# The attention layer's input product in 24 steps of seven products, W_v split beside the weight fusion, and one q, k, v tile loaded ahead

## What is computed

```
h = x @ w_in                       # 1024 x 3088: q 512, k 512, v 1024, g 1024, lr 16
gk = log_sigmoid(lr @ w_gk + b_gk) / 16          # per head, summed along each chunk
qe = q * exp(cumsum(gk)) ; ke = k * exp(-cumsum(gk)) ; kd = k * exp(last - cumsum(gk))
o = tril(qe @ ke.T) @ v + qe @ state             # state from chunk to chunk
y0 = (rmsnorm(o) * norm_w * silu(g)) @ w_out     # then a layer norm of ALPHA * x + y0
layer 1: h = x @ w_in ; causal means of u over 2, 4, 8, 16 rows ; @ w_grp ; * silu(z) ; @ w_out
```

## Time and profile before

| | us |
|---|---|
| median of three runs | 2005.64 |
| the profiled execution | 2001.48 |
| its span | 1999.6 |
| `prepare` to its last matmul | 132.3 |
| v in `project` | 132.3 to 313.0 |
| gate columns | 313.0 to 329.6 |
| four heads | 329.6 to 690.7 |
| start of `attend_and_norm`, to its first output product | 690.7 to 724.2 |
| last stage, its first matmul of a step | 1041.5 |

### The profile page before, as it was taken

How to read it: one execution, slowest core, us unless ns; L and a number is a source line. 1 busy time by engine, 2 the same in 40 slices (tenths; PEclk the granted TensorE clock), 3 DMA queues, 4 the chain that set the end, 5 groups by cost and what they waited for, 6 DMA issues and landing times.

```text
span 1999.6 us, 24456 instructions
## 1 busy us (share of the span) xinstructions
PE 1914.5 (96%) x8974; PEld 1588.5 (79%) x8974; DVE 1161.7 (58%) x1539; ACT 701.3 (35%) x1065; POOL 431.5 (22%) x268
## 2 busy tenths in 40 slices
PE   8999999999999989999949999999999999999997
PEld 7778887888888778888738888887888886787786
DVE  4330102332415277787675688868678657546998
ACT  4441213131313243343354444344434335224331
POOL 0005200000000000000043666423334343322430
PEclk9999999999999999999979999999999999999999
DMA  8766530334233464455322444333322225647342
GB/s 254 221 202 239 178 103 17 108 87 118 79 101 87 159 242 164 172 187 170 136 96 74 153 141 152 135 104 137 129 88 73 94 74 193 249 170 272 129 177 95
DMA packets 229912, 287.74 MB, mean 144 GB/s; under 512 B 17216, under 2 KB 170176, under 8 KB 227904
## 3 DMA queue, kind: packets, MB, share of 16 engines
q1 hardware_dynamic: 225216, 278.20, 42.0%
q10 hardware_dynamic: 4608, 8.39, 1.1%
HBM read 186.93 MB, written 99.61 MB: 143 GB/s over the span
## 4 chain that ended last, share of the span: by engine, by line
PE 41%; DVE 4%; issue 4%; ACT 1%; POOL 0%; DVEq 0%; POOLq 0%; ACTq 0%
PE banks L165 13%; PE banks L166 13%; PE banks L167 13%; DVE m_w_lo L1922 1%; DVE m_x_lo L1936 1%; ACT m_x_hi L1728 0%; DVE m_x_lo L1914 0%; PE banks L1621 0%; PE banks L1668 0%; DVE m_stats L2025 0%; DVE m_x_lo L1896 0%; DVE m_res L2019 0%; DVE m_res L2035 0%; POOL m_s L1859 0%; DVE m_win_b L1968 0%
## 5 line engine op out<-in xcount | busy, mean ns | idle before, releaser
L165 PE MATMUL banks<-m_x_hi,m_w_hi 128*128 128x512 f32 x1320 | 517.6, 392 | 9.4 <-DVE m_res L2019 3.5
L166 PE MATMUL banks<-m_x_lo,m_w_hi 128*128 128x512 f32 x1320 | 515.3, 390 | 0.0
L167 PE MATMUL banks<-m_x_hi,m_w_lo 128*128 128x512 f32 x1320 | 515.0, 390 | 0.0
L165 PEld LDWEIGHTS banks<-m_x_hi,m_w_hi 128*128 128x128 f32 x1320 | 248.7, 188 | 63.7 <-DVE m_w_lo L1922 10.0
L166 PEld LDWEIGHTS banks<-m_x_lo,m_w_hi 128*128 128x128 f32 x1320 | 248.8, 188 | 52.0 <-issue 0.7
L167 PEld LDWEIGHTS banks<-m_x_hi,m_w_lo 128*128 128x128 f32 x1320 | 248.7, 188 | 52.0
L1854 POOL TENSOR_TENSOR m_s<-pair_raw 128x512 f32<-128x512 f32 x24 | 47.3, 1969 | 891.6 <-POOLq L947 757.5
L165 PE MATMUL banks<-x_hi,h_w_hi 128*128 128x512 f32 x512 | 199.9, 390 | 0.8 <-DVE h_g_out L833 0.8
L166 PE MATMUL banks<-x_lo,h_w_hi 128*128 128x512 f32 x512 | 199.3, 389 | 0.0
L167 PE MATMUL banks<-x_hi,h_w_lo 128*128 128x512 f32 x512 | 199.3, 389 | 0.0
L1716 ACT ACTIVATE m_w_hi<-m_s 128x512 fp32r<-128x512 f32 x184 | 115.5, 629 | 202.7 <-PE banks L167 179.2
(11 more groups left out here) (220 smaller groups left out, 3117.7 us busy)
## 6 DMA issues: line engine op xcount, KB each, us to landing
p_in<-in_pool_w_in SPq DMA_DIRECT2D x32, 256.0 KB, 4.9
p_rows<-in_x SPq DMA_DIRECT2D x16, 512.0 KB, 5.2
w_fused<-p_out SPq DMA_DIRECT2D x32, 256.0 KB, 3.9
h_out_rows<-in_pool_w_out SPq DMA_DIRECT2D x16, 512.0 KB, 6.7
v_tiles<-v_out ACTq DMA_DIRECT2D x32, 256.0 KB, 2.1
w_terms<-h_out_terms SPq DMA_DIRECT2D x8, 1024.0 KB, 5.6
h_raw<-in_gla_w_in SPq DMA_DIRECT2D x16, 512.0 KB, 4.2
g_tiles<-h_g_out SPq DMA_DIRECT2D x32, 256.0 KB, 2.3
```

Source lines behind the costliest of these rows:

```text
L165: nc.tensor.matmul(out, a_hi, b_hi, start=first, stop=False, skip_group_check=True)
L166: nc.tensor.matmul(out, a_hi, b_lo, start=False, stop=False, skip_group_check=True)
L167: return nc.tensor.matmul(out, a_lo, b_hi, start=False, stop=last, skip_group_check=True)
```

## The change

`project` is rewritten in the form of the last stage. There are 24 steps of seven products in place of all full products. Steps 0 to 7 make v: the stationary operand is a pair of x tiles, the moving one the seven blocks of W_v. Then the seven blocks are exchanged for those of the first half of x's rows (1024), and steps 8 to 15 make one head's q and k (`qk`) or one head's g (`g`) each, in the order of `UNITS`; they are exchanged again for the second half and steps 16 to 23 follow. The seven blocks are `b_hi`, `b_lo` and `b_raw`, the last two in the same memory, so that a block can be loaded only when its product of the last step before the exchange is done. None is loaded ahead and none is multiplied unsplit. In steps 8 to 23 the moving operand is read as four runs of 128 columns, 512 floats apart (`moving`). GpSimd forms four sums of weights in each step.

A head's work is cut in two halves of 1024 columns, and tables say in which step and after which product each part stands (`Q_AT`, `KEYS_AT`, ...; (7, 3) is step 7 of eight, after product 3, and -1 is ahead of product 0). x goes through DRAM (`x_in`): eight tiles are transposed in `prepare`, beside every fourth fusion tile, and eight in steps 0 to 3. VectorE forms the sums of x blocks in steps 0 to 7. The seven blocks of W_v are loaded, summed by GpSimd (16 sums of 128 x 512) and split in `prepare`, from fusion tile 18 on. The gate columns are done once per half (`rank_rows`): 80 matmuls in place of 64. `w_fused` is stored as a plain matrix. SP loads q, k, v of the first row tile in step 23 and of the second only in `attend_and_norm`, ahead of `gla_w_out`. The sums of `pool_w_out` move from `project` to steps 17 to 24 of the last stage.

```diff
-        self.w_fused = scratch("w_fused", [MT, P, KT, P])
+        self.w_fused = scratch("w_fused", [D, POOL_W])
+        self.x_in = scratch("x_in", [2, 8, P, KT // 2, BLK])
...
-        self.x_hi = self.place("x_hi", [P, KT, SEQ], F32R)
-        self.x_lo = self.place("x_lo", [P, KT, SEQ], F32R)
+        self.b_hi, self.b_lo, self.b_raw = {}, {}, {}
+        for j in ORDER:
+            self.b_hi[j] = self.place(f"b_hi{j}", [P, HALF_K, BLK], F32R)
+            at = self.at
+            self.b_lo[j] = self.place(f"b_lo{j}", [P, HALF_K, BLK], F32R)
+            self.at = at
+            self.b_raw[j] = self.place(f"b_raw{j}", [P, HALF_K, BLK])
...
+    V_PARTS = {1: 4, 7: 8, 5: 12, 3: 12, 6: 16, 2: 16, 4: 16}
+    FIRST_PART = 18
+    PAIR_AT = 26
...
-            return n // 2 if n % 2 else None
+            return n // 4 if n % 4 == 1 else None
...
+                b11, b12, b22, b21 = (p.b_raw[j] for j in V_LOADS)
+                t1, t2, t3, t4 = (p.b_raw[j] for j in (5, 6, 7, 4))
+                for j in (1, 7):
+                    pool.wait_ge(b_loaded[j], DMA)
+                for k in range(HALF_K):
+                    nc.gpsimd.tensor_tensor(t1[:, k, :], b12[:, k, :], b11[:, k, :], ALU.subtract).then_inc(b_summed, 1)
...
+                    if n >= FIRST_PART:
+                        j, rows = part(n)
+                        act.wait_ge(b_summed, V_PARTS[j])
+                        nc.scalar.activation(p.b_hi[j][:, rows, :], p.b_raw[j][:, rows, :], ACT.Copy).then_inc(b_hi_done, 1)
...
+    UNITS = (("g", 0), ("g", 1), ("qk", 0), ("qk", 1), ("g", 2), ("qk", 2), ("qk", 3), ("g", 3))
...
+    Q_AT = {0: (3, -1), 1: (4, 2), 2: (6, -1), 3: (7, 2)}
+    KEYS_AT = {0: ((3, 0), (2, 5)), 1: ((4, 3), (4, 4)), 2: ((6, 1), (6, 0)), 3: ((7, 3), (7, 5))}
+    TURN_KEYS_AT = {0: (3, 2), 1: (4, 6), 2: (6, 3), 3: (7, 6)}
...
+    TURN_HI = {0: (0, 3), 1: (0, 4), 2: (0, 5), 3: (1, -1), 4: (1, 0), 5: (1, 1), 6: (1, 2)}
+    TURN_LO = {0: (0, 4), 1: (0, 5), 2: (1, -1), 3: (1, 0), 4: (1, 1), 5: (1, 2), 6: (1, 3)}
...
+            def load_x(e, n):
+
+                sp.wait_ge(product_mm, 7 * (e * EPOCH - 1) + n + 1)
+                sp.dma_start(x_raw[ORDER[n]][:], p.x_in[e - 1, (0, 1, 3, 7, 4, 5, 6)[ORDER[n] - 1]]
+                             ).then_inc(x_loaded[n], DMA)
...
+            def product(i, n):
+                j = ORDER[n]
+                pe.wait_ge(w_lo_done, PRODUCTS * i + n + 1)
+                if i and i % EPOCH == 0:
+                    pe.wait_ge(x_lo_done, turns_to(i // EPOCH, n))
+                if n == 0 and i < 2:
+                    nc.tensor.matmul(bank(i, 6), w_hi[1][:, 0, :], x_hi[1][:, 0, :], start=True, stop=True)
+                free(i, j)
+                opens = j in (1, 5)
+                for k in range(HALF_K):
+                    last = split_product(nc, shaped(i, bank(i, j)), w_hi[j][:, k, :], w_lo[j][:, k, :],
+                                         moving(i, x_hi[j], k), moving(i, x_lo[j], k), opens and k == 0, k == HALF_K - 1)
+                last.then_inc(product_mm, 1)
+
...
+            def turn_keys(m):
+
+                for n in range(2):
+                    pe.wait_ge(k_done[n], m + 1)
+                for n in range(2):
+                    for c in range(HALF_K):
+                        t = n * HALF_K + c
+                        last = nc.tensor.transpose(p.ps[:, 6 + n, c * P:(c + 1) * P], sums[:, t * P:(t + 1) * P], p.ident[:])
...
+            def turn_hi(e, n):
+
+                j = ORDER[n]
+                act.wait_ge(x_loaded[n], e * DMA)
+                act.wait_ge(product_mm, PRODUCTS * (e * EPOCH - 1) + n + 1)
+                nc.scalar.activation(x_hi[j][:], x_raw[j][:], ACT.Copy).then_inc(x_hi_done, 1)
...
+            def turn_lo(e, n):
+
+                j = ORDER[n]
+                dve.wait_ge(x_hi_done, turns_to(e, n))
+                nc.vector.tensor_tensor(x_lo[j][:], x_raw[j][:], x_hi[j][:].bitcast(F32), ALU.subtract
+                                        ).then_inc(x_lo_done, 1)
...
+                    if i == STEPS - 1 and n == 0:
...
+                        p.load_qkv(sp, 0, 0)
...
+            for s, n in enumerate((6 * 4, 2 * 4)):
+                sp.wait_ge(p.g_stored[s], n * DMA)
+            for stored, n in ((p.q_stored, 2), (p.k_stored, 4), (p.kn_stored, 2)):
+                sp.wait_ge(stored, 2 * HEADS * n * DMA)
+            p.load_qkv(sp, 1, 1)
...
+                if 0 <= i - FIRST_OUT_CHUNK - 1 < OUT_CHUNKS:
+                    out_sums(i - FIRST_OUT_CHUNK - 1)
```

1226 lines of the change are left out of this document (800 added, 426 removed).

## The result

The changed kernel takes 2007.53 us (median of 20 runs, 2004.71 to 2012.02 but for one slow run of 6603 us, which the ratio leaves out), the kernel before 2003.49 in its 20 runs beside it. The ratio is 1.0018 with a 95% interval of 1.0011 to 1.0025: 2 to 5 us slower. The forecast was 1979 with a range of 1962 to 1996; the time lies above it, in the stretch (2001.6 to 2009.6) to which the prediction gave a chance of 0.02. The profiled execution has a span of 2003.4 us against 1999.6.

What follows compares the result with a forecast made beforehand. TensorE was taken as the bound, its stages adding up. From the profiled 2001.48 us, -65.3 + 4.1 - 6.4 + 27.4 + 7.5 + 6 + 0.5 = -26.2 gave 1975.3; with 4.2 for the median, 1979, range 1962 to 1996.

Steps and rivals of the forecast that it cites:

- A: Matmuls that go in v and the heads: 288 fewer at 0.2267 us each, -65.3 us.
- R4: Rival: TensorE reads four runs of 128 columns more slowly in steps 8 to 23, 2010 us; chance 0.04.
- B: Matmuls that come: 16 gate matmuls and two opening an accumulation, +4.1 us; eight x tiles changing stage count nothing.
- C: Waits that go: v_lo 4.0, h_rank 1.6, h_g_out 0.8, together -6.4 us.
- D: New waits in `project`: start 9, first exchange 3, second exchange 12, smaller ones 3.4, together +27.4 us.
- the prediction's own sign for D: The whole would be wrong if the waits in `project` summed to under 15 us or above 45.
- R2: Rival: VectorE is behind all along in `project`, slowed by GpSimd's sums, 1 us in 14 steps, 1993 us; chance 0.15.
- E: `prepare`: copies of W_v by ScalarE delay fusion tiles, and loads land late, +7.5 us (2 to 15).
- F: Start of attention: second tile's loads ahead of `gla_w_out` and the last keys' store, +6 us (3 to 9).
- G: Last stage: GpSimd's 32 sums of `pool_w_out` hidden, `w_fused` read in 512 B runs, +0.5 us (-1 to +4).
- R1: Rival: copies and subtractions keep up, so the waits are hidden, about 1962 us; chance 0.20.
- R3: Rival: loading of the seven blocks bounds the exchanges, 2.9 us more at each, 1985 us; chance 0.07.

Runs made afterwards that it cites:

- the thin sums: Changed kernel with GpSimd's weight sums in `project` cut to one column of 128 from step 2 on, other work left out; ratio 0.9938 to the kernel before.
- `moves_and_sums`: Changed kernel with five orders of loads, stores, copies and key transposes mended and VectorE forming `project`'s weight sums from step 2: 1975.4 us, ratio 0.9870 to kernel before.

## Why the prediction was wrong, step by step

- **A, right.** 288 matmuls went, at a pitch of 0.2267, as the count shows: steps 4 to 7, 10, 18 and 23 took 19.04 us each; the others have waits, transposes or gates in them. Steps 10, 18 and 23 read four runs of 128 columns. So R4 is out: they cost TensorE nothing.
- **B, 1.7 short:** the gate matmuls took 18.8 us for 15.0 and the two that open an accumulation 0.8, 4.6 in all where 4.1 was forecast; the eight x transposes took 0.94 each in their new place and not 0.79, 1.2 us more.
- **C, right:** those waits went.
- **D, the failed term.** Forecast 27.4, measured 46: 33 us of waits, and 13 us more of half clock than before against 1.7 forecast. Of the waits the second exchange was right in place and order: 5.0 and 7.1 us, less an eighth, 10.5 in sum, were forecast, and 5.9 and 4.5, 10.4, measured at the two places named. That the sums agree is in part luck: the working had nothing for GpSimd's sums beside VectorE, and with these thinned the two waits are 3.8 and 3.6, 7.3 in sum. Missed was the wait for x's rows (6.1, and 0.8 behind it), which the sum had as nothing: SP's order was not followed there. The load stands behind a wait for VectorE's sums of x in step 0, which is in the code. The start was 3.3 and not 9, the first exchange 4.5 and not 3, the keys and small ones 7.6 and not 3.4.
- **The clock, mis-sized.** The prediction charged it once, behind the second exchange. It fell behind each of the long waits: at the start, behind x's rows, behind both exchanges. This also shows what the prediction's own sign for D was worth: the waits' sum, 32.9, lies between its bounds of 15 and 45, and the term was missed all the same, since the matmuls behind a wait are in no sum of waits.
- **The weighing of GpSimd against VectorE, read wrong.** The prediction took 0.79 us for a subtraction, a mean over the whole kernel that hid 0.69 alone and up to 1.79 beside a GpSimd sum. It set this effect aside in R2, since the last stage has no gap with four sums a step. But a stage that hides the effect between its exchanges doesn't hide it at one. R2 priced it at 14 us and the thin sums give 16 back; that these are near each other is luck, for R2 spread it as 1 us over each of 14 steps, and it came at the exchanges and before the keys, with steps of 19.04 between. The Trainium skill, GPSIMD Engine Reference, section Specifications, says that contention arises with VectorE instructions that have two SBUF inputs; by that rule, the runs agree, down to the additions with a PSUM operand that were not slowed. The runs decided what the prediction had left as a row that speaks against it.
- **E, mis-sized.** Forecast 7.5, measured 9.8 (3.5 longer with the 6.3 of the transposes gone). The three waits for ScalarE were there (1.2 each, forecast 1.6). Of the other 6 us 5.5 are waiting, the waits of 2.8 and 5.9 behind late stores where the kernel before lost 3.0 in all, and the rest is half clock. The working's own terms, three times 1.6 and as much again for loads that land late, make 9.6 and not the 7.5 that it took.
- **F, two terms short.** Forecast 6, measured 8.6: the bytes were counted, but not SP's 2.7 us to issue five loads, nor all of its six stores ahead of the barrier (3.2 instead of 1.6). What ends the stretch stays open, as said above.
- **G, wrong.** Forecast 0.5 and "hidden"; measured 5.3, in one step: 4.2 more of waiting at the first exchange and half clock behind it. Its sum for GpSimd was off too, eight sums a step of 2.03 being 16.2 us and not 12.2, but GpSimd was not what ran short. That GpSimd has time says nothing on what its work does to VectorE: the sums were hidden on GpSimd and not on VectorE at the exchange.
- R1 was wrong in D. R3 was not seen: the long waits at the exchanges ended with VectorE, which was busy 24.0 of the 24 us up to the end of the first one's wait (310 to 334); ScalarE waited 1.6 us for a load in them.

The miss of 30 us is thus 20 in `project` (7 waits, 11 clock, 2 transposes and gates), 5 in the last stage, 3 at the start of attention, 2 in `prepare`. The saving of the algorithm, 65 us, is real; the schedule around it gave it back. Some 30 us of it came back by order alone and by who forms the sums, which puts `moves_and_sums` 26 us below the kernel before.

## What to carry to other kernels

When work moves from the engine that bounds to its helpers, sum each helper's row between two points that the bounding engine waits for, with durations split by what ran beside them: the mean of 0.79 us over the whole kernel hid that one in four lasted 1.09. For every new gap of some us count also the matmuls behind it at half clock, as a chance and not as a certainty. And a step that is moved is late by the waits and issues of the queue that it stands in, which are read from the order of that queue, not from its busy share.
